# The three products of one k side by side: a new order of matmuls in the output and feed-forward projections of a hybrid decoder step

## The reference

```python
h = rmsnorm(x, norm1_g)
z = h @ w_in                      # u, c, b, q, k, v, o, gates: 8 heads
... short convolution and chunked mLSTM ...
mix = sigmoid(g_a) * a_out + sigmoid(g_b) * b_out
x = x + mix @ w_out               # 2048 x 2048
h2 = rmsnorm(x, norm2_g)
up, fc = causal_dwconv(h2 @ w_up, fc0, w_ffconv)          # 2048 x 11264
x = x + (silu(up[..., D_FF:]) * up[..., :D_FF]) @ w_down  # 5632 x 2048
y = rmsnorm(x, norm_f_g)
```

## Time and profile before

| | us |
|---|---|
| median of 3 runs | 1713.26 |
| lowest and highest | 1712.54, 1713.76 |
| profiled execution, its own time | 1713.21 |
| its span, first to last instruction | 1711.5 |
| TensorE busy | 1700.5 |
| VectorE busy | 1201.9 |
| ScalarE busy | 766.6 |
| GpSimd busy | 475.6 |

### The profile page before, as it was taken

The page is one execution under the profiler, slowest core; times in us unless marked ns, Lnnn a source line. Parts: engine busy times, 40 slices in busy tenths (PEclk is TensorE's granted clock), DMA queues, the critical chain, the costliest instruction groups (busy, mean ns, idle before and its releaser), DMA issues.

```text
span 1711.5 us, 37177 instructions
## 1 busy us (share of the span) xinstructions
PE 1700.5 (99%) x13726; PEld 1694.0 (99%) x13726; DVE 1201.9 (70%) x1901; ACT 766.6 (45%) x916; POOL 475.6 (28%) x501
## 2 busy tenths in 40 slices
PE   9999999999999999999999999999999999999997
PEld 8999999999999999999999999999999999999997
DVE  5875957667595866759688877777555777777554
ACT  6544435353443535444444544544333333334443
POOL 4422414242151424215333222222000222222220
PEclk9999999999999999999999999999999999999999
DMA  8787786868778686877766666666666666666663
GB/s 201 184 230 197 198 212 156 224 164 229 183 196 214 154 227 158 232 185 199 192 174 183 188 172 181 177 180 173 181 181 181 179 176 181 172 182 174 183 178 120
DMA packets 591165, 318.80 MB, mean 186 GB/s; under 512 B 17684, under 2 KB 585988, under 8 KB 588988
## 3 DMA queue, kind: packets, MB, share of 16 engines
q1 hardware_dynamic: 578564, 292.99, 63.7%
q10 hardware_dynamic: 10448, 21.57, 4.9%
q0 software_dynamic: 2064, 2.92, 0.8%
HBM read 305.09 MB, written 12.78 MB: 186 GB/s over the span
## 4 chain that ended last, share of the span: by engine, by line
PE 99%; ACT 0%; POOL 0%; DVE 0%; issue 0%; ACTq 0%; POOLq 0%; DVEq 0%
PE strip L1520 63%; PE strip L1525 32%; PE aux L1398 1%; PE aux L1406 1%; PE strip L1450 0%; PE aux L1578 0%; PE aux L1470 0%; PE strip L1463 0%; PE aux L1608 0%; PE aux L1607 0%; PE aux L1621 0%; PE strip L1398 0%; PE aux L1612 0%; PE aux L1605 0%; PE aux L1613 0%; PE aux L1614 0%
## 5 line engine op out<-in xcount | busy, mean ns | idle before, releaser
L977 DVE TENSOR_TENSOR w_lo<-w_raw,w_hi 128x1024 fp32r<-128x1024 f32 x556 | 721.6, 1301 | 316.8 <-ACT w_hi L708 316.3
L708 ACT ACTIVATE w_hi<-w_raw 128x1024 fp32r<-128x1024 f32 x557 | 586.4, 1059 | 764.4 <-PE strip L1525 734.0
L1520 PE MATMUL strip<-xh,w_hi 128*128 128x268 f32 (+2 forms) x3424 | 863.8, 286 | 0.0
L1520 PE MATMUL strip<-xl,w_hi 128*128 128x268 f32 (+2 forms) x3424 | 862.9, 286 | 0.0
L1520 PEld LDWEIGHTS strip<-xh,w_hi 128*128 128x128 f32 x3424 | 644.9, 188 | 0.2
L1520 PEld LDWEIGHTS strip<-xl,w_hi 128*128 128x128 f32 x3424 | 644.5, 188 | 0.0
L1525 PE MATMUL strip<-xh,w_lo 128*128 128x268 f32 (+2 forms) x3424 | 495.1, 287 | 0.0
L1525 PEld LDWEIGHTS strip<-xh,w_lo 128*128 128x128 f32 x3424 | 451.9, 189 | 0.2 <-DVE w_lo L977 0.2
L1520 PE MATMUL strip<-hh,w_hi 128*128 128x264 f32 x704 | 176.2, 285 | 0.0
L1520 PE MATMUL strip<-hl,w_hi 128*128 128x264 f32 x704 | 174.8, 283 | 0.0
L679 POOL TENSOR_TENSOR gg<-sg,cz 128x264 f32<-128x264 f32 x44 | 57.3, 1302 | 415.0 <-ACT sg L922 415.0
(11 more groups left out here) (324 smaller groups left out, 1335.2 us busy)
## 6 DMA issues: line engine op xcount, KB each, us to landing
w_raw<-in_w_in SPq DMA_DIRECT2D x256, 512.0 KB, 4.4
w_raw<-in_w_up SPq DMA_DIRECT2D x176, 512.0 KB, 4.1
w_raw<-in_w_down SPq DMA_DIRECT2D x64, 512.0 KB, 3.9
w_raw<-in_w_out SPq DMA_DIRECT2D x32, 512.0 KB, 4.4
w_raw<-in_w_down SPq DMA_DIRECT2D x32, 384.0 KB, 3.3
out<-c_st ACTq DMA_DIRECT2D x8, 1024.0 KB, 7.0
c_st<-in_state_mlstm_C ACTq DMA_DIRECT2D x7, 1024.0 KB, 10.9
rb<-scratch_rows ACTq DMA_DIRECT2D x8, 270.0 KB, 5.0
```

What stands on the lines that cost most here:

```text
L708: act.activation(w_hi[:, slot, :], w_raw[:, slot, :], ACT.Copy).then_inc(hi_done, 1)
L977: v.tensor_tensor(w_lo[:, slot, :], w_raw[:, slot, :], w_hi[:, slot, :].bitcast(f32), ALU.subtract).then_inc(lo_done, 1)
L1520: pe.matmul(bank[b][:, 0:c1 - c0], w_hi[:, slot, w], xt[:, k0 + k, c0:c1], start=(first and k == 0 and t == 0), stop=False)
```

## The change

A second unit function, `unit_by_tile`, has both waits at its begin and then, for each k, the two high products and the low product. The output projection, up-projection and down-projection use it. The mixing stage keeps `unit`.

```diff
+            def unit_by_tile(u, slot, b, k0, kk, rh, rl, c0, c1, first, last, waits=(), frees=1):
+                pe.wait_ge(hi_done, u + 1)
+                pe.wait_ge(lo_done, u + 1 + RING)
+                for k in range(kk):
+                    for at_k, sm, value in waits:
+                        if at_k == k:
+                            pe.wait_ge(sm, value)
+                    w = slice(k * P, (k + 1) * P)
+                    for t, xt in enumerate((rh, rl)):
+                        pe.matmul(bank[b][:, 0:c1 - c0], w_hi[:, slot, w], xt[:, k0 + k, c0:c1],
+                                  start=(first and k == 0 and t == 0), stop=False)
+                    mm = pe.matmul(bank[b][:, 0:c1 - c0], w_lo[:, slot, w], rh[:, k0 + k, c0:c1],
+                                   start=False, stop=(last and k == kk - 1))
+                if frees:
+                    mm.then_inc(unit_used, frees)
...
-            def strip(s, u, i, b, rh, rl, c0, c1, need=(), between=None):
+            def strip(s, u, i, b, rh, rl, c0, c1, need=(), between=None, of_unit=unit_by_tile):
...
-                    unit(u + h, (i + h) % RING, b, h * KU, KU, rh, rl, c0, c1, h == 0, h == 1, waits)
+                    of_unit(u + h, (i + h) % RING, b, h * KU, KU, rh, rl, c0, c1, h == 0, h == 1, waits)
...
             def mix_strip(n, s, c0, c1, between=None):
-                strip(n * 16 + s, n * HEAD_U + 2 * s, 2 * s, s % RING, xh, xl, c0, c1, (), between)
+                strip(n * 16 + s, n * HEAD_U + 2 * s, 2 * s, s % RING, xh, xl, c0, c1, (), between, unit)
...
             def out_unit(q, h, waits, frees):
-                unit(U_B + 2 * q + h, 2 * q + h, q, h * KU, KU, mh, ml, 0, NM, h == 0, h == 1, waits, frees)
+                unit_by_tile(U_B + 2 * q + h, 2 * q + h, q, h * KU, KU, mh, ml, 0, NM, h == 0, h == 1, waits, frees)
...
-                    unit(u + h, (3 * q + h) % RING, q, k, kk, hh, hl, 0, NF, h == 0, h == len(DOWN_UNITS) - 1, waits)
+                    unit_by_tile(u + h, (3 * q + h) % RING, q, k, kk, hh, hl, 0, NF, h == 0, h == len(DOWN_UNITS) - 1, waits)
```

## The result

| | before | changed |
|---|---|---|
| median, us | 1713.36 (8 runs) | 1717.66 (8 runs) |
| lowest and highest | 1712.53, 1714.57 | 1716.72, 1719.54 |
| profiled execution, span | 1711.5 | 1715.5 |

The ratio is 1.0027 with a 95% interval of 1.0018 to 1.0035: the change made the kernel slower, by 4.3 us. The forecast was 1713 us with no change that can be told as the likeliest case; the time lies inside its range of 1706 to 1719, but it moved the other way than the likeliest case had it: what came true is the rival of looser starts, which had 0.17.

What follows compares the result with a forecast made beforehand. The prediction took the number of TensorE matmuls and how densely they start as the bound. Its four steps, 0 + 0 + 0 + 0 on the profiled execution's 1713.21 us, gave 1713 us, range 1706 to 1719.

Steps and rivals of the forecast that it cites:

- rival of looser starts: Feed-forward matmuls start less densely, at the output projection's 13.1 ns over the columns: 1721 us, chance 0.17.
- Step 1: Wait for w_lo 16 matmuls sooner in each unit; every wait met before it is reached, 2.1 us to spare: cost 0.
- Step 2: Up to 304 semaphore instructions of 51 ns at units' begins, hidden under 2.2 us of queued matmuls: cost 0, at most 15.5 us.
- Step 3: Waits at a later k give the last tiles 0.25 to 0.86 us more, but they were not late: gain 0.
- Step 4: New order of 7104 matmuls alters the remainder over their columns: taken as 0, between 8.5 us less and 7.8 us more.

Runs made afterwards that it cites:

- e1: Kernel before with both waits moved to the unit's begin, products in the order of before: 1712.97 us, ratio 0.9998.
- e4: Changed kernel with the mixing stage using the new unit as well: 1730.75 us.
- e2: Changed kernel with the wait for the low part two matmuls later, at the unit's first low product: 1719.23 us, ratio 1.0030.
- e5: Changed kernel with products in groups of 4 k in the output projection and first feed-forward half, groups of 2 k in the second: 1717.68 us.
- e7: Changed kernel with every product of a unit reading one x tile in the first feed-forward half, the same weight columns in the second: 1723.67 us.
- e8: Order of before, every product of a unit reading one x tile in the first feed-forward half, the same weight columns in the second: 1715.25 us.
- e13: Order of before, up-projection's moving columns read 4 columns further on in the first half, 8 in the second: 1714.31 us.
- e14: Order of before, up-projection's moving columns read 12 columns further on in the first half, 14 in the second: 1714.99 us.
- e9: Order of before, up-projection streaming 268 columns in the first half and 272 in the second instead of 266: 1721.99 us.
- e10: Changed kernel's order, up-projection streaming 268 columns in the first half and 272 in the second instead of 266: 1719.92 us.
- e15: Changed kernel's order, up-projection's moving columns read 4 columns further on in the first half, 8 in the second: 1720.15 us.
- e3: Changed kernel with the low product between the two high ones for each k, both waits at the begin: 1718.76 us.
- e11: Order of before with a small extra matmul ahead of each up strip but the first, 8 columns then 64 by half: 1725.03 us.
- e12: Changed kernel's order with a small extra matmul ahead of each up strip but the first, 8 columns then 64 by half: 1729.04 us.

## Why the prediction was wrong

**What bounds the kernel** was right: matmuls times their distance. All of the change stands in the counts by window, none in waits. Two readings of short windows were off, since a count in them is good to one matmul only: by the begins, the units of 280 columns have 128.9 ns a matmul, not 128.0, and the stretch from 557.5 us 12.2 ns over its columns, not 12.5. Neither is a bound of the sum.

**Step 1, the earlier wait** was right at 0: e1 has it and runs at 0.9998, and TensorE has no wait for line 977. In the output and feed-forward projections the 2 us of cover were real; e4 shows what it costs where they are missing.

**Step 2, the added instruction** was right at 0 and wrong in number. What line 1534, the wait for w_lo, issues in TensorE's queue (ns min/median/max, first and last start):

```profile
L1534 PEldq ALU_OP  x228: 32/32/42, 846.4 to 1567.0; - x114
L1534 PEldq EVENT_SEMAPHORE  x69: 51/51/51, 831.3 to 1699.5; - x69
```

69 semaphore instructions more, not 304; the seven of before now stand at line 1538. In the other 228 units the value waited for is computed by a register operation (as it was before, at line 1522), and no semaphore instruction shows. That one of the two waits rides on this operation is inferred, not shown. The Trainium skill ("TensorE: Matmul & The Clock Gate", section "Wait — 56ns, not 53.3ns?") puts about 62 ns of the sequencer on a matmul when hardware decoding is off, and the prediction's estimate from it was 19 us for 304 entries. No run shows whether decoding is off here, but e1, with the 69 entries and no loss, does not agree with a price of that kind: 69 x 62 ns would be, as an estimate, 4.3 us, and its ratio is 0.9998 (0.9989 to 1.0007).

**Step 3, the waits at a later k** found nothing to gain, and nothing was gained; it had no run of its own.

**Step 4, the order itself** is the step that failed, in "neither pure runs of low products nor pairs of high ones stand out in the rows, so I take 0". The mechanism it named is what happened, the remainder over the columns depends on how the loads and matmuls fall; its size was taken as 0 and measured +0.83 ns for each of the 4224 matmuls of the up-projection (+3.5 us) and +0.5 to +0.7 ns for each of the 2112 of the down-projection (+1.3 us). Both lie within the bounds of the step, 7.8 us at the most. The prediction had priced the up-projection at the output projection's 13.1 ns with +3.8 us, and the up-projection came out at just 13.1; that this value and not another one came is luck, since nothing in the rows picked it. The rival of looser starts had put its decision at 0.48 ns over all; it was 4.8 us / 7104 = 0.67 ns. Could the sign have been read from before? The rows had 12.2 ns for the up-projection in an observed span of 10.8 to 13.1, so neither side was favoured, and the experiments say why: at other widths the same change of order has the other sign, and at another place a third of the size.

**What is shown and what stays open.** Shown: the cost is that of the order (e1, e2); it is not a price for each change between high and low weights (e5), nor does it come from the place of the weights (e7, e8) or from the layout of the instructions (e13, e14); it depends on the place and the width of the moving rows (e9, e10, e13 to e15) and on the phase handed on (e3, e11, e12). Open: the rule by which order, place and width give the length. None of the tables predicts a cell that was not measured. Meanwhile SyncE's transfers, ScalarE and VectorE write w_raw, w_hi and w_lo, and no run took that away. That the lengths repeat to within 1 ns speaks against a part of theirs, and is all there is on it.

## What to carry to other kernels

Where TensorE has no waits, the time is the number of matmuls times their distance, and this distance has a part over its columns (here 11 to 13 ns of 123, a tenth of the kernel) that depends on order, width and the place of the moving rows. In the kernels that read every tile once, a new order at the same width and place changed a unit by -0.3% (three passes in the output projection) to +0.9%. So count matmuls in windows by stage, beside the busy share, and measure a reordering rather than take it as free. Waits that are met 2 us ahead cost nothing, whether one or two; where the cover is thin, as in the mixing stage, pulling a wait 16 matmuls forward made TensorE wait for 9.2 us and the stage end 13.6 us later.

## What the runs showed of the hardware

The length that settled in the loops was a multiple of 6.67 ns in every run: up units of 440, 443, 444, 445, 446, 447, 452 and 456 times that, first-half down strips of 1200 (8000 ns), 1202, 1206, 1207, 1208 and 1220, two output units of 892 (5946.7), and with the small matmul strips of 902 (6013.3), 910 and 912. In e14 (column 14) and e10 (272 columns) it is two units that make a multiple, 889 and 902. 6.67 ns are 16 columns at one column a cycle of 2.4 GHz. The single distances in a unit are as a rule not multiples of it; away from the small matmul they scatter from 115 to 135 ns and repeat to within 1 ns. With the x tile held and the new order each of them is one: 126.7 ns, 19 times 6.67. And one loop body can have two lengths: 2973 and 2980 ns in the two halves of e3, 2973 and 2940 ns in two stretches of each head before.
